# Where the first partial sums of a feed-forward block's weights come from, and the order of two engines' work in a block

## What is computed

```
x += 0.5 * FFN1(rms(x));  x += Mixer(rms(x));  x += 0.5 * FFN2(rms(x))
FFN(h) = (silu(h @ w_gate) * (h @ w_up)) @ w_down      # 1024 -> 2816 -> 1024
```

## Time and profile before

| | us |
|---|---|
| median of 3 runs | 2507.07 |
| the three runs | 2506.56, 2507.07, 2524.66 |
| the profiled execution | 2519.46 |
| its span | 2517.6 |
| PE busy in the span | 2346.6 |
| VectorE (DVE) busy | 1657.7 |
| ScalarE (ACT) busy | 1165.5 |
| GpSimd (POOL) busy | 487.6 |

### The profile page before, as it was taken

How to read it: one execution, slowest core, us unless ns; L and a number is a source line. 1 busy time by engine, 2 the same in 40 slices (tenths; PEclk the granted TensorE clock), 3 DMA queues, 4 the chain that set the end, 5 groups by cost and what they waited for, 6 DMA issues and landing times.

```text
span 2517.6 us, 47212 instructions
## 1 busy us (share of the span) xinstructions
PE 2346.6 (93%) x17889; PEld 2254.5 (90%) x17889; DVE 1657.7 (66%) x2599; ACT 1165.5 (46%) x2162; POOL 487.6 (19%) x342
## 2 busy tenths in 40 slices
PE   7798999999999999999898999899999999899998
PEld 7798899976899999999898999898999999789898
DVE  7776765556455555547876667867766656877764
ACT  4445444364455555534445444445544223444542
POOL 0333330000000000000333330343430000334340
PEclk9999999989999999999999999899999999999999
DMA  4677764311111111203676664577773333577772
GB/s 136 157 179 185 182 173 125 87 47 30 45 44 47 49 45 42 60 26 93 168 191 175 179 167 119 134 184 193 185 181 101 90 93 93 134 184 185 190 195 85
DMA packets 417696, 313.29 MB, mean 124 GB/s; under 512 B 34624, under 2 KB 372630, under 8 KB 417480
## 3 DMA queue, kind: packets, MB, share of 16 engines
q1 hardware_dynamic: 401748, 253.66, 34.0%
q0 software_dynamic: 15552, 56.63, 12.9%
q10 hardware_dynamic: 180, 0.11, 0.0%
HBM read 194.27 MB, written 2.87 MB: 78 GB/s over the span
## 4 chain that ended last, share of the span: by engine, by line
PE 19%; DMA 15%; DVE 7%; issue 4%; POOL 4%; ACT 2%; DVEq 0%; ACTq 0%; SPq 0%; POOLq 0%
DMA wsum75b<-raw 7%; PE ps L552 4%; PE ps L556 4%; PE ps L554 4%; DMA raw<-in_w_ffn_up 3%; PE ps L946 2%; DMA wsum<-raw 2%; PE ps L948 2%; PE ps L947 2%; POOL wsum L734 2%; DMA raw<-in_w_ffn_down 2%; POOL wsum L732 2%; DVE w_lo L683 1%; ACT w_hi L669 1%; DVE hs L778 1%
## 5 line engine op out<-in xcount | busy, mean ns | idle before, releaser
L946 PE MATMUL ps<-hs,w_hi 128*128 128x260 f32 x1440 | 417.0, 290 | 65.1 <-ACT gate_t L1013 25.5
L947 PE MATMUL ps<-hs,w_hi 128*128 128x260 f32 x1440 | 411.4, 286 | 0.0
L948 PE MATMUL ps<-hs,w_lo 128*128 128x260 f32 x1440 | 411.1, 285 | 0.0
L946 PEld LDWEIGHTS ps<-hs,w_hi 128*128 128x128 f32 x1440 | 275.6, 191 | 77.6 <-DVE w_lo L673 38.8
L947 PEld LDWEIGHTS ps<-hs,w_hi 128*128 128x128 f32 x1440 | 276.4, 192 | 0.0
L948 PEld LDWEIGHTS ps<-hs,w_lo 128*128 128x128 f32 x1440 | 275.8, 192 | 0.0
L2071 ACT ACTIVATE ksq<-ps 128x384 f32<-128x384 f32 (+1 forms) x384 | 146.8, 455 | 196.6 <-PE ps L2024 196.6
L946 PE MATMUL ps<-hs,x_hi 128*128 128x260 f32 x688 | 202.2, 294 | 34.8 <-DVE x_lo L653 13.9
L734 POOL TENSOR_TENSOR wsum<-wsum,raw 128x512 f32<-128x512 f32 x108 | 206.3, 1911 | 8.5
L947 PE MATMUL ps<-hs,x_hi 128*128 128x260 f32 x688 | 198.3, 288 | 0.0
L948 PE MATMUL ps<-hs,x_lo 128*128 128x260 f32 x688 | 198.2, 288 | 0.0
(11 more groups left out here) (409 smaller groups left out, 6410.3 us busy)
## 6 DMA issues: line engine op xcount, KB each, us to landing
raw<-in_w_ffn_gate SPq DMA_DIRECT2D x88, 512.0 KB, 4.1
raw<-in_w_ffn_up SPq DMA_DIRECT2D x88, 512.0 KB, 3.9
raw<-in_w_ffn_down SPq DMA_DIRECT2D x64, 512.0 KB, 4.5
wsum<-raw SPq DMA_DIRECT2D x56, 512.0 KB, 3.5
wsum<-raw POOLq DMA_DIRECT2D x56, 512.0 KB, 4.8
wsum75b<-raw SPq DMA_DIRECT2D x52, 512.0 KB, 3.4
wsum75b<-raw POOLq DMA_DIRECT2D x52, 512.0 KB, 5.0
cache<-in_cache_latent SPq DMA_DIRECT2D x128, 128.0 KB, 2.0
```

Source lines behind the costliest of these rows:

```text
L946: nc.tensor.matmul(o, hi[:, kc], mh[:, xc], start=start and k == 0, stop=False, skip_group_check=goes_on)
L947: nc.tensor.matmul(o, hi[:, kc], ml[:, xc], start=False, stop=False, skip_group_check=goes_on)
L948: mm = nc.tensor.matmul(o, lo[:, kc], mh[:, xc], start=False, stop=k == KH - 1, skip_group_check=goes_on)
```

## The change

In sums_begin the copy within SBUF becomes two loads of 256 KB from DRAM: the first four chunks of the first tile and of the second tile go straight into the two halves of sums(). SP no longer waits there for the tiles. It does wait, from the second such block on, until the adding DMA of the block before has landed (sums_added). sums_begin is issued between the loads of row 0 and row 1. GpSimd takes over the waits for both tiles, ahead of its adding DMA. On ACT keep_second moves ahead of the pair's rounding. On DVE pair_mix moves behind second_made and first_begun ahead of pair_lo.

```diff
-        def sums_begin(sp, bk):
-
-            for j in range(2):
-                bk.loaded(sp, j)
+        def sums_begin(sp, bk, first, second):
+
             if bk.b == 4:
                 sp.wait_ge(set_made, own_sets(bk.at, KH))
                 sp.wait_ge(part_used, blocks[bk.at][2].done)
             elif bk.b > 4:
                 sp.wait_ge(part_lo_made, blocks[bk.at][bk.b - 2].end(M75, 2))
-            r = bk.raw_slot(0)
-            sp.dma_start(bk.sums()[:].rearrange("p (h c) -> p h c", h=2), raw[:, r:r + 2, 0:bk.width]).then_inc(sums_in, 16)
+            if bk.s:
+                sp.wait_ge(sums_added, 16 * bk.s)
+            dst = bk.sums()[:].rearrange("p (h k c) -> p h k c", h=2, c=P)
+            sp.dma_start(dst[:, 0], first[:, 0:KH, :]).then_inc(sums_in, 16)
+            sp.dma_start(dst[:, 1], second[:, 0:KH, :]).then_inc(sums_in, 16)
...
-            pool.wait_ge(sums_in, 16 * (bk.s + 1))
+            for j in range(2):
+                bk.loaded(pool, j)
+            pool.wait_ge(sums_in, 32 * (bk.s + 1))
             pool.dma_start(bk.sums()[:], bk.raw_row(1), accum_op=ALU.add).then_inc(sums_added, 16)
...
+            def weights(bk, j):
+                if bk.out:
+                    return dw[:, BASES[bk.c]:BASES[bk.c] + KD, (2 * bk.d + j) * P:(2 * bk.d + j + 1) * P]
+                return (gw, uw)[j][:, :, bk.f * P:(bk.f + 1) * P]
+
             for bk in blocks[at][1:]:
                 for j in range(bk.loads):
+                    if j and bk.kind in "SD":
+                        sums_begin(sp, bk, src, weights(bk, 1))
                     if bk.raw + j >= RAW:
                         raw_free(sp, bk.raw + j)
...
-                    if bk.out:
-                        k0, d0 = BASES[bk.c], (2 * bk.d + j) * P
-                        src = dw[:, k0:k0 + KD, d0:d0 + P]
-                    else:
-                        src = (gw, uw)[j][:, :, bk.f * P:(bk.f + 1) * P]
+                    src = weights(bk, j)
                     sp.dma_start(bk.raw_row(j).rearrange("p (k c) -> p k c", c=P), src).then_inc(weights_in[bk.raw_slot(j)], 16)
-                if bk.kind in "SD":
-                    sums_begin(sp, bk)
...
                 m4_hi(act, bk)
+                keep_second(bk)
                 if done:
                     last_hi(act, done) if done.last else pair_hi(act, done)
-                keep_second(bk)
...
                 if early:
                     after(old)
-                    if done and not done.last:
-                        pair_mix(dve, done)
                 m75_lo(dve, bk)
                 second_made(bk)
-                m4_lo(dve, bk)
                 if not early:
+                    m4_lo(dve, bk)
                     pair_mix(dve, done)
                     first_begun(bk)
                     pair_lo(dve, done)
                     first_lo(dve, nxt)
                     plain_hid(old)
                 else:
+                    if done and not done.last:
+                        pair_mix(dve, done)
+                    m4_lo(dve, bk)
+                    first_begun(bk)
                     if done:
                         last_lo(dve, done) if done.last else pair_lo(dve, done)
-                    first_begun(bk)
                     plain_lo(dve, nxt) if nxt.plain else first_lo(dve, nxt)
```

## The result

The changed kernel is slower: 2554.67 us (median of 4) against 2513.84 us for the kernel before on the same chip (median of 4), a ratio of 1.0165, 95% interval 1.0115 to 1.0215, about 41 us by the medians. The forecast was 2441, with a range of 2405 to 2500. It went to the other side, as the rival on SP's wait had it, at less than half that rival's price.

A forecast was written before the change was run, and what follows sets the result against it. PE was taken to wait on the sums, whose two-block round of 22.86 us set 11.35 a block. At 10.7, 96 blocks save 62 us, FFN starts 4 more: from 2507 to 2441 us, range 2405 to 2500.

The forecast's parts named there:

- the rival on SP's wait: Sums' loads on SP: row 1 lands late behind the wait, round 12.5 us, 110 us slower, 2617; chance 0.12.
- What bounded the kernel before: FFN blocks: PE waits some 122 us in 96 blocks, mostly ending with keep_first; a two-block round sets 11.35 us a block.
- item 1: Copy leaves the old two-block round: 22.86 falls to 19.6 us, 9.8 a block, below PE's 10.08.
- Items 2 and 3: New one-block round between adding DMA landings: 5.7 us until row 1 lands, adding DMA alone at 4.6, 10.64 in all.
- The rival of the slow adding DMA: Adding DMA on GpSimd stays at 5.1 to 5.2 us: round 11.24, 2492 us, no difference that counts; chance 0.20.
- Its second mechanism: GpSimd writes the adding DMA's descriptors over a port VectorE can lock, so an empty queue would not make it faster.
- Item 6: keep_second and DVE order: nothing gained beyond the FFN starts; a possible slip of 0.25 us a block counted as none.
- The rival for this: DVE and ACT order holds PE in pair blocks: mean pace 10.9 us, gain 47 us, 2460; chance 0.15.
- Item 5: Start of each FFN: about 1 us gained by block 5, 4 us in all, at most 2 lost each.
- C: Theory at the start of the experiments, on DRAM loads: the 57 MB more read made loads late.
- The signs named in the prediction: Profile after: 250 to 260 us per FFN, adding DMA near 4.6, row 1 landing 5.4 to 5.8 after first issue.

The follow-up runs named there:

- row 1 first: The changed kernel with row 1's load issued ahead of the sums' loads, SP's wait kept: 2474.53 us, ratio 0.9885 to the kernel before.
- no wait: The changed kernel without SP's wait for the adding DMA, each sums buffer with its own landing semaphore: 2470.27 us, ratio 0.9871 to the kernel before.
- loads alone: The changed kernel with the old order on ACT and DVE, the two DRAM loads and SP's wait kept: 2549.78 us, ratio 1.0189 to the kernel before.
- the order alone: The kernel before with only the new order on ACT and DVE, the copy within SBUF kept: 2531.75 us against 2507.93, ratio 1.011.

## Why the prediction was wrong, point by point

**What bounded the kernel before** was right, and so was item 1: with the copy out of the way (row 1 first, or no wait) the pace falls below 11.0, and 31 to 46 us are won. One reading was off: of the 122 us that PE waits, give 45.4 to keep_first, which is the largest share and not "most".

**Items 2 and 3, the new round, are where it failed: its terms were mis-sized.** The round exists, and it is the pace. The forecast summed 0.05 + 5.7 + 0.29 + 4.6 = 10.64. Over the 100 blocks in which SP stood at the wait, the start and landing times in the two traces give these means (us):

| term | forecast | changed | loads alone |
|---|---|---|---|
| SP's reaction | 0.05 | 0.06 | 0.06 |
| first issue to row 1's landing | 5.7 | 6.30 | 6.32 |
| GpSimd's reaction | 0.29 | 0.55 | 0.55 |
| the adding DMA | 4.6 | 4.93 | 4.74 |
| round | 10.64 | 11.85 | 11.67 |

All the terms err to one side, and the middle one by the most. In the chain of the changed kernel:

- From the first issue to row 1's landing 1681.52 - 1675.53 = 5.99, and 0.06 of reaction before it. I took 5.7 and argued that the extra issue was hidden. Row 1's load goes out 1.01 after the first issue (0.37, 0.50 and two gaps), not 0.70, and lands 4.98 after that; the median landing of up loads is 5.2, which makes 6.2. With 5.1 in the earlier trace rows, that leaves nothing of the later issue hidden. The row that I built on had a copy within SBUF ahead of the load, and this has two loads from DRAM. Over 3.5 us of each the DMA engines moved (DMA share and GB/s last; the first row is of the kernel before, the second of the changed one):

```profile
1237.00:1240.50 3.50, 2.67 (x23) 2.49 (x22) 2.83 (x5) 2.77 (x5) 0.25 (x1) 1.00 1.00 295
```

```profile
1677.00:1680.50 3.50, 2.11 (x17) 1.90 (x17) 2.96 (x4) 0.00 (x0) 3.35 (x2) 1.00 0.93 268
```

  By these rates 1.05 MB takes 3.55 us and 3.91, 0.36 more. This is another view of the same lateness, not a term to be added to the later issue: the share of 0.93 says that the engines were not fully busy in the second window. The prediction weighed the rule of the Trainium skill (DMA: Bandwidth & Descriptors, Bandwidth) for this, HBM side against fabric, and set it aside as smaller than the spread. The direction here is the rule's; how much of the 0.6 is the source of the data and how much the later issue, no run separates.
- GpSimd's reaction is 0.54 instead of 0.29, and it is 0.5 in 97 of the 100 blocks. GpSimd now waits for two tiles and the sums' loads, where it waited for the copy. Which of its waits makes the 0.25 was not tried.
- The adding DMA: 4.7 in the median (4.5 at least, 7.4 at most) where I had 4.6, but 5.00 and 5.29 in the chain shown. "It runs alone" holds only where GpSimd's sums are done early; here they took 2.59 and 2.15, row 0's load of the next block went out late, and it overlapped. The rival of the slow adding DMA was right in part. Its second mechanism, GpSimd held up by VectorE, isn't seen: with the loads alone, VectorE as busy as before, the landing fell from 4.9 to 4.6 in the median, and it is 5.7 where loads run beside it (no SP wait), so it moves with the loads. The section of the Trainium skill that the prediction cites there (SBUF — State Buffer, "SBUF: two separate sides") ties that lock to VectorE's 2-port modes. The prediction took VectorE's busy time for the condition.

The terms come to 0.06 + 6.0 + 0.54 + 5.3 = 11.9 in this turn. The means, 11.85 and 11.67, stand against paces of 11.76 and 11.61. The errors of 0.6, 0.26 and 0.1 to 0.3 in one round had the same sign each time. Since the old pace (11.35) was only 0.7 away, that was enough to turn the sign. The two columns differ by 0.18 a block, all of it in the adding DMA: as far as one execution each can tell, the order reaches the round through it. That was not tested by itself.

**Item 6 failed on "I take none".** The pair block was worked out at 11.7 us (its terms add up to 11.76) and called covered. It is 13.2 from keep_first to keep_first (12.3 before). The sum left out that L653 takes 2.30 beside GpSimd's additions, not 1.2, and that keep_first of the next block slips with it. The block after doesn't take the slip back: others stay at 11.0 with the order alone. The rival for this had the right mechanism, but as a smaller gain; alone it is a loss of 24 to 27 us. Its count was off too: pair_mix runs in 8 of the 27 blocks (3, 4, 6, 8, 14, 16, 18, 20), not 11.

**Item 5** was wrong by 3 us an FFN: from block 3's keep_first to block 5's it is 29.9 us in the mean of the four FFNs, 28.0 before, where I had 27. Block 4 is a pair block too, and both parts lose there: it is 29.7 with the order alone and 29.0 with the loads alone. The 0.7 us that item 5 expected from first_begun and pair_lo changing places can't come in block 3, whose order on DVE the diff leaves as it was.

**The rival of SP's wait** named the mechanism, the place and the point of decision (a round over 11.35, slower by 1% from 11.6), and all three hold. Its price of 12.5 came from the longest load of the chain; the round is 11.6 to 11.9. Its chance of 0.12 was too small: against it stood one row, of a copy and a load. C, which I had not listed as a rival, is excluded by the run without the wait. The signs named in the prediction did their work. As expected, SP waits for the adding DMA in nearly every block, 57 MB more are read, and L1022 no longer holds PE. Against it, the FFNs' 24 periods take 280 to 284 us instead of 250 to 260, PE waits for L653, row 1 lands 6.2 us behind the first issue in the median and over 6.5 in 20 of 100 blocks, and the adding DMA, 4.7 in the median, is at 5 or more in 36 of them.

## What to carry to other kernels

A wait on a queue costs what is issued behind it. Before moving an issue past a wait, ask what stands next in that queue and how long a round it closes: here the same wait was harmless with one load moved ahead of it, and cost about 3% without. When a new round is within 10% of the old pace, don't take each term near its best row: here all the errors had one sign. And an engine's order can be moved only where nobody waits at the end of it; a mix that was moved one place made either ACT's copy or DVE's last subtraction late.

## What the runs showed of the hardware that was not expected

The 128x1024 subtraction L653 takes 1.2 us alone and up to 2.4 beside GpSimd's additions, and these take up to 3.2 instead of 1.3 then, as at 1675.62 above. The kernel before has it too; two L653, and the two additions that ran beside the first:

```profile
1648.49 1.31 POOL L732 TENSOR_TENSOR wsum<-wsum75b,raw 128x512 f32<-128x512 f32 x1 [4.31 <-DMA wsum75b<-raw]
...
1648.79 2.09 DVE L653 TENSOR_TENSOR w_lo<-raw,w_hi 128x1024 fp32r<-128x1024 f32 x1 [0.80 <-ACT w_hi L649]
...
1649.87 2.16 POOL L734 TENSOR_TENSOR wsum<-wsum,raw 128x512 f32<-128x512 f32 x1
...
1661.12 1.22 DVE L653 TENSOR_TENSOR x_lo<-raw,x_hi 128x1024 fp32r<-128x1024 f32 x1
```

They don't slow each other down evenly, they take turns. L732 began first and took its 1.31 as if alone; L653 ends 1.08 after it, at 1650.88; L734 ends 1.15 after that, at 1652.03. So it is throughout: wherever an L653 began while an addition ran, 63 times in the kernel before and 51 in the changed one, it ended 1.08 to 1.09 us after that addition; an addition that began while a DVE instruction with both inputs in SBUF ran, 137 and 111 times, ended 1.12 to 1.18 us after it; and the 29 that began while DVE worked with an operand in PSUM kept their 1.3 us. Each makes the other late, so a late DVE chain also delays the next block's sums. The Trainium skill (SBUF — State Buffer, "SBUF: two separate sides") says that the two engines share one pair of ports, which one of them holds for a whole instruction; these ends agree.

The adding DMA, 4.7 in the median while SP held back row 1's load and the sums', lands in 5.7 with these free to run beside it (run without SP's wait), and the kernel is 3% faster than the changed one all the same.
